# x by features from the host, latents turned off TensorE, early products with v: one kernel of a hybrid encoder trunk

## What is computed

```python
for l in range(DEPTH):                                   # DEPTH = 2
    h = rms_norm(x, norm_g[l])
    p = h @ w_in[l]                                      # 2048 x (2048 + 2112 + 2176 + 6144)
    ...                                                  # A) stick-breaking attention, 4 heads
    c_q, c_kv, k_rope, mg = split_cols(p_mla, (Q_LORA, KV_LORA, MLA_ROPE, MLA_WIDTH))
    q = (rms_norm(c_q, mla_q_norm_g[l]) @ mla_w_uq[l])   # B) latent attention: latents 512 wide
    kv = (rms_norm(c_kv, mla_kv_norm_g[l]) @ mla_w_ukv[l])
    ...
    prev = jnp.pad(rw_main, ((0, 0), (1, 0), (0, 0)))[:, :-1]
    rw_main = rw_main + rw_mu[l] * (prev - rw_main)      # C) RWKV-7: mixes each token with the one before
    rr, rk, rv, wd, ad = split_cols(rw_main, (RW_WIDTH,) * 3 + (DECAY_LORA, ICL_LORA))
    ...                                                  # per head: state <- state*w + sa*b + v*k; out = state.r
    merged = (g_sb * (y_sb @ w_br_sb[l]) + g_mla * (y_mla @ w_br_mla[l]) + g_rw * (y_rw @ w_br_rw[l]))
    x = x + merged @ w_out[l]
```

## Time and profile before

| | us |
|---|---|
| median of 3 runs | 1691.61 |
| lowest, highest | 1690.33, 1692.4 |
| the profiled execution, its own time | 1692.25 |
| its span, first to last instruction | 1690.5 |
| TensorE busy | 1677.6 |
| VectorE, ScalarE, GpSimd busy | 1134.9, 836.6, 487.8 |

### The profile page before, as it was taken

The page is one execution under the profiler, slowest core; times in us unless marked ns, Lnnn a source line. Parts: engine busy times, 40 slices in busy tenths (PEclk is TensorE's granted clock), DMA queues, the critical chain, the costliest instruction groups (busy, mean ns, idle before and its releaser), DMA issues.

```text
span 1690.5 us, 22088 instructions
## 1 busy us (share of the span) xinstructions
PE 1677.6 (99%) x8394; PEld 1399.2 (83%) x8394; DVE 1134.9 (67%) x1579; ACT 836.6 (49%) x1181; POOL 487.8 (29%) x722
## 2 busy tenths in 40 slices
PE   8999999999999999999999999999999999999999
PEld 7878888888888888888888788888888888888887
DVE  5668575766976566886656775756669666578853
ACT  6454453435544455554454454434445554555532
POOL 1011212410343426362410112233203534244500
PEclk9999999999999999999999999999999999999999
DMA  8865655655666557785687555556556565668754
GB/s 277 243 193 182 175 177 170 184 165 173 178 184 176 173 164 234 236 302 188 205 269 226 176 186 172 187 152 188 174 167 178 167 178 177 192 212 279 267 193 157
DMA packets 176913, 332.82 MB, mean 197 GB/s; under 512 B 19516, under 2 KB 32746, under 8 KB 176808
## 3 DMA queue, kind: packets, MB, share of 16 engines
q1 hardware_dynamic: 167048, 297.86, 57.7%
q0 software_dynamic: 9584, 33.48, 5.7%
q10 hardware_dynamic: 176, 0.07, 0.0%
HBM read 311.20 MB, written 16.78 MB: 194 GB/s over the span
## 4 chain that ended last, share of the span: by engine, by line
PE 92%; DVE 3%; ACT 2%; DMA 2%; issue 1%; SPq 1%; ACTq 0%; DVEq 0%
PE D L707 83%; PE B L707 8%; DMA ring<-in_w_in 2%; DVE w_lo L1398 1%; ACT w_hi L1026 1%; DVE xy L1398 0%; ACT arena L1026 0%; ACT gev L1026 0%; PE B L898 0%; DVE arena L1398 0%; DVE gev L1444 0%; PE B L877 0%; SPq L435 0%; ACT L1026 0%; DVE arena L1428 0%
## 5 line engine op out<-in xcount | busy, mean ns | idle before, releaser
L1398 DVE TENSOR_TENSOR w_lo<-ring,w_hi 128x1024 fp32r<-128x1024 f32 (+3 forms) x560 | 675.7, 1219 | 342.1 <-ACT w_hi L1026 334.0
L1026 ACT ACTIVATE w_hi<-ring 128x1024 fp32r<-128x1024 f32 (+3 forms) x560 | 575.0, 1038 | 463.9 <-PE D L707 361.5
L707 PE MATMUL D<-w_hi,ht_hi 128*128 128x512 f32 (+2 forms) x1728 | 681.3, 394 | 3.0 <-DVE w_lo L1398 2.8
L707 PE MATMUL D<-w_hi,ht_lo 128*128 128x512 f32 (+2 forms) x1728 | 666.0, 385 | 0.0
L707 PE MATMUL D<-w_lo,ht_hi 128*128 128x512 f32 (+2 forms) x1728 | 665.1, 385 | 0.0
L707 PEld LDWEIGHTS D<-w_hi,ht_hi 128*128 128x128 f32 x1728 | 325.1, 188 | 71.4 <-issue 7.8
L707 PEld LDWEIGHTS D<-w_hi,ht_lo 128*128 128x128 f32 x1728 | 324.5, 188 | 65.3
L707 PEld LDWEIGHTS D<-w_lo,ht_hi 128*128 128x128 f32 x1728 | 325.2, 188 | 59.0 <-issue 0.5
L609 POOL COPY arena<-arena 32x256 f32<-32x256 f32 x240 | 163.1, 680 | 144.7 <-DVE arena L1428 109.3
L707 PEld LDWEIGHTS B<-arena 128*66 128x66 f32 (+3 forms) x1312 | 134.2, 165 | 24.3 <-issue 8.2
L707 PE MATMUL B<-arena 128*66 128x64 f32 (+7 forms) x1312 | 144.7, 263 | 0.6 <-ACT arena L1026 0.6
(11 more groups left out here) (160 smaller groups left out, 1376.9 us busy)
## 6 DMA issues: line engine op xcount, KB each, us to landing
ring<-in_w_in SPq DMA_DIRECT2D x368, 512.0 KB, 4.5
ring<-in_w_out SPq DMA_DIRECT2D x64, 512.0 KB, 5.2
ring<-in_w_br_mla SPq DMA_DIRECT2D x32, 512.0 KB, 5.2
gate_spill<-gev POOLq DMA_DIRECT2D x24, 512.0 KB, 4.7
arena<-gate_spill POOLq DMA_DIRECT2D x24, 512.0 KB, 5.2
ring<-in_mla_w_ukv SPq DMA_DIRECT2D x16, 512.0 KB, 4.0
ring<-in_w_br_rw SPq DMA_DIRECT2D x16, 512.0 KB, 5.2
ring<-in_w_br_sb SPq DMA_DIRECT2D x16, 512.0 KB, 5.2
```

Source lines behind the costliest of these rows:

```text
L707: return nc.tensor.matmul(o, a, b, start=start, stop=stop, skip_group_check=True)
L1026: return nc.scalar.activation(o, i, fn, **kw)
L1398: return v.tensor_tensor(o, a, b, op)
```

## The change

Four things, in one kernel.

1. **x by features.** The host passes x transposed as well (`xt`) and the gains as columns (`gain_cols`). SyncE loads the four blocks of `xt` at the place of x; ScalarE and VectorE make ht_hi and ht_lo straight from them. TensorE's 32 transposes and its product with the gains go. x by rows, needed for the squares and the residual, is loaded ahead of chunks 9 to 12, and the squares stand behind the splits of chunks 12 to 15. `AT_LORA` is 17 instead of 16.
2. **Latents turned by VectorE and GpSimd.** Behind the normalising, VectorE transposes c_q and c_kv within blocks of 32 x 32 (two instructions), GpSimd moves the blocks to their places with 32 copies in groups of four (`move_latents`), during pairs 1 and 2, and ScalarE and VectorE split them ahead of pair 3 (`latents_hi`, `latents_lo`). TensorE's 16 transposes a layer go, with its wait before pair 1.
3. **Early products with v.** They are issued in the second visit of the last level, into B[0] and a part of B[3]; ScalarE copies the first half's there. A pair has 20 visits instead of 21, and the steps are spread anew.
4. **Transfers.** The rows of gains and the low-rank matrices are loaded ahead of chunk 20 instead of 12 (both layers), the constants by GpSimd after the shift of rk instead of after that of wk.

```diff
 AT_MIX = [END[n] + 3 for n in ("rr", "rk", "rv")]
-AT_LORA = END["wk"] + 8
+AT_LORA = END["wk"] + 9
...
-RW_STEPS = [1, 1.2, 1, 1.5, 1.8] + [0.88, 0.98] * LEVELS + [0.85] * 6
-LATENT_STEPS = [2, 2.5]
+RW_STEPS = [1, 1.2, 1, 1.5, 1.8] + [0.9, 1] * LEVELS + [0.98] * 5
+LATENT_STEPS = [1.2, 1.1, 1.3, 1.2]
...
-STEPS = RW_STEPS + LATENT_STEPS + 3 * RW_STEPS + GN_STEPS + ML_STEPS + SBH // 2 * SB_STEPS
+STEPS = RW_STEPS + LATENT_STEPS[:2] + 2 * RW_STEPS + LATENT_STEPS[2:] + RW_STEPS + GN_STEPS + ML_STEPS + SBH // 2 * SB_STEPS
...
         at_mkv = used[0]
+        XT = [arena[:, j * 1024:(j + 1) * 1024] for j in range(3)] + [arena[:, at_mkv:at_mkv + 1024]]
+        XT = [t.rearrange("p (k t) -> p k t", k=4) for t in XT]
         CQ, CKV = again(at_mkv, lambda: halved(1024), lambda: halved(1024))
+        LAT_TURNED = [S1, PV[:, :, 512:1024]]
+        LAT_MOVED = [t.rearrange("p h c -> p (h c)").rearrange("p (k t) -> p k t", k=4) for t in (CQ, CKV)]
...
             for j in range(4):
-                first_x(j)
+                sp.dma_start(XT[j], xt[j].rearrange("p (k t) -> p k t", k=4)).then_inc(xt_in[j], 16)
...
+                    if l == 0 and 2 * RING < n <= 3 * RING:
+                        first_x(n - 2 * RING - 1)
...
                         row(MU[:, 0:1536], rw_mu[l, 0:1536], mu_in[1][l])
-                    if n == 3 * RING:
+                    if n == 5 * RING:
...
                 shift(PW, WK[:, :, 64:192], wk_shift[l])
-                if l == 0:
-                    pool.wait_ge(split_lo, END["wk"] + 2)
-                    pool.dma_start(con[:, P:K_END], consts[:, P:K_END]).then_inc(con_in, 16)
                     shift(PV[:, :, i * 512:(i + 1) * 512], R[:, :, i * 512:(i + 1) * 512], r_shift[i][l])
+                    if l == 0 and i == 1:
+                        pool.dma_start(con[:, P:K_END], consts[:, P:K_END]).then_inc(con_in, 16)
...
+                def move_latents(i, d):
+                    turned = LAT_TURNED[i].rearrange("p h (k j t) -> p h k j t", k=4, j=4)
+                    moved = LAT_MOVED[i].rearrange("p k (h i t) -> p h k i t", h=2, i=4)
+                    if d == 0:
+                        pool.wait_ge(lat_turned, 2 * l + i + 1)
+                    for i0 in range(4):
+                        j = (i0 + d) % 4
+                        nc.gpsimd.tensor_copy(moved[32 * j:32 * j + 32, :, :, i0, :],
+                                              turned[32 * i0:32 * i0 + 32, :, :, j, :]).then_inc(lat_quarters, 1)
+                    pool.wait_ge(lat_quarters, 16 * (2 * l + i) + 4 * d + 4)
+                    if d == 3:
+                        pool.sem_inc(lat_moved, 1)
                 for p in range(4):
-                    if p == 1:
-                        beat(len(LATENT_STEPS))
+                    if p in (1, 3):
+                        beat(2)
...
                     pool.wait_ge(rw_pool, 4 * RW_POOL * l + RW_POOL * p + 7)
+                    if p in (1, 2):
+                        move_latents(p - 1, 0)
                         beat(2)
+                        if p in (1, 2):
+                            pool.wait_ge(rw_pool, 4 * RW_POOL * l + RW_POOL * p + 7 + n)
+                            move_latents(p - 1, n)
+                    if p in (1, 2):
+                        move_latents(p - 1, 3)
...
                     beat(6)
-                    beat(6)
+                    beat(5)
...
                     pe.wait_ge(rw_dve, 4 * RW_DVE * l + d0)
-                if p == 1:
-                    pe.wait_ge(lat_out[l], 16)
...
                     pe.wait_ge(rw_act, 4 * RW_ACT * l + a0 + 1 + n)
+                    if n == LEVELS:
+                        for h in range(HALVES):
+                            v = R[:, h, 1024 + p * P:1024 + (p + 1) * P]
+                            for a in range(2):
+                                mm((B[0], B[3])[h][:, h * P + 64 * a:h * P + 64 * a + 64], AM[:, 2 * a + h, 256:384],
+                                   v[:, 64 * a:64 * a + 64], a == 0, True)
...
                     if h:
-                        mm(B[0][:, 0:P], TT[:, 1, 0:P], ST, True, False)
-                    for a in range(2):
-                        last = mm(B[0][:, own[a]], AM[:, 2 * a + h, 256:384], v[:, own[a]], h + a == 0, True)
-                    last.then_inc(rw_pe, 1)
-                    beat()
+                        mm(B[3][:, P:2 * P], TT[:, 1, 0:P], ST, False, True).then_inc(rw_pe, 1)
+                        beat()
...
-            def latents():
-                beat()
-                pe.wait_ge(rw_dve, 4 * RW_DVE * l + RW_DVE)
-                pe.wait_ge(lat_dve[l], 1)
-                for i, s in enumerate((CQ, CKV)):
-                    for k in range(4):
-                        for h in range(HALVES):
-                            o = B[2 * i + k // 2][:, k % 2 * 256 + h * P:k % 2 * 256 + (h + 1) * P]
-                            last = nc.tensor.transpose(o, s[:, h, k * P:(k + 1) * P], ident)
-                    last.then_inc(lat_pe[l], 1)
-                beat()
...
-            pe.wait_ge(id_in, 16)
                 if l == 0:
-                    pe.wait_ge(gain_rows, 16)
-                    mm(D[3][:, 0:KD], NG16, ident[0:KD, 0:KD], True, True).then_inc(gain_columns, 1)
-                    for j in range(4):
-                        pe.wait_ge(x_moved[j], 16)
-                        if j >= 2:
-                            pe.wait_ge(first_xl, 2 * j - 2)
-                        transposes((2 * j, 2 * j + 1), j * 512, first_pe)
-                        if j:
-                            dense_to(2 * j)
+                    dense_to(END["wk"])
+                    pe.wait_ge(id_in, 16)
...
                     beat()
+                    if n == LEVELS:
+                        act.wait_ge(rw_pe, 4 * RW_PE * l + e + 2 * LEVELS + 2)
+                        f(YU[:, 0:P], B[0][:, 0:P]).then_inc(rw_act, 1)
                 for h in range(HALVES):
-                    for k in range(2):
-                        act.wait_ge(rw_pe, 4 * RW_PE * l + e + 2 * LEVELS + 3 + 3 * h + k)
-                        f(YU[:, k * P:(k + 1) * P], B[k][:, 0:P]).then_inc(rw_act, 1)
+                    for k in range(1 - h, 2):
+                        act.wait_ge(rw_pe, 4 * RW_PE * l + e + 2 * LEVELS + 2 + 3 * h + k)
+                        f(YU[:, k * P:(k + 1) * P], B[1][:, 0:P] if k else B[3][:, P:2 * P]).then_inc(rw_act, 1)
...
                 f(css, css, ACT.Exp, scale=-0.5).then_inc(lat_act[l], 1)
-                beat()
+                beat(2)
+            def latents_hi():
+                act.wait_ge(small_in[l], gains(l))
                 for i, (t, g) in enumerate(((cqh, cqg), (ckh, ckg))):
-                    act.wait_ge(lat_pe[l], i + 1)
-                    act.wait_ge(small_in[l], gains(l))
+                    act.wait_ge(lat_moved, 2 * l + i + 1)
                     for k in range(4):
-                        f(t[:, k, :], B[2 * i + k // 2][:, k % 2 * 256:(k % 2 + 1) * 256], scale=g[:, k:k + 1]
-                          ).then_inc(lat_hi[l], 1)
-                beat()
+                        f(t[:, k, :], LAT_MOVED[i][:, k, :], scale=g[:, k:k + 1]).then_inc(lat_hi[l], 1)
+                    beat()
...
                 if l == 0:
-                    first_split(0)
-                    columns_hi(0, first_pe, first_xh)
-                    first_split(1)
-                    columns_hi(1, first_pe, first_xh)
-                    first_split(2)
-                    first_squares(0)
-                    dense_to(1)
-                    first_squares(1)
-                    columns_hi(2, first_pe, first_xh)
-                    dense_to(3)
-                    first_squares(2)
-                    columns_hi(3, first_pe, first_xh)
-                    dense_to(5)
-                    first_squares(3, 4)
-                    dense_to(6)
-                    first_squares(5, 6)
-                    dense_to(7)
-                    first_squares(7)
-                    at[0] = END["wk"]
-                    split(END["wk"] + LEAD - 1)
+                    for c in range(KD // KC):
+                        first_columns_hi(c)
+                        if c < LEAD:
+                            first_split(c)
+                        else:
+                            dense_to(c + 1 - LEAD)
+                    dense_to(END["wk"] - 1)
+                    while at[0] < END["wk"] + 5:
+                        at[0] += 1
+                        split(at[0] + LEAD - 1)
+                        if at[0] > END["wk"] + 1:
+                            first_squares(2 * (at[0] - END["wk"]) - 4, 2 * (at[0] - END["wk"]) - 3)
...
                         latents()
+                    if p == 3:
+                        latents_hi()
...
                         last = v.tensor_scalar(t[:, h, :], t[:, h, :], css[:, 2 * i + h:2 * i + h + 1], None, ALU.mult)
-                last.then_inc(lat_dve[l], 1)
-                beat()
+                link(last)
```

(26 more changed lines are left out.)

79 lines of the change are left out of this document (39 added, 40 removed).

## The result

The changed kernel takes 1696.72 us (median of 7 runs, 1696.26 to 1699.2), the kernel before 1691.93 us in the same comparison. The ratio is 1.0034, with a 95% interval of 1.0023 to 1.0045: it is slower by 0.34% (the two medians alone give 0.28%). The profiled execution has a span of 1695.6 us, 5.1 us more than before.

The account below looks back on a forecast made before the run. TensorE bounds the kernel, so only its work or waits in the first 37 us count: -3.6 - 0.3 - 0.6 + 6.4 = +1.9 us, giving a median of 1693.5 us; range 1687.5 to 1697.0, the forecast's own 1690.3 to 1695.0.

Parts of the forecast that it names:

- The chain of the start: Layer 0's start: late squares delay GpSimd's shift, VectorE's mixing and TensorE's transposes, so chunk 17 begins at 57.0 us.
- GpSimd and VectorE in the pairs: Latent copies on GpSimd and normalising, turning and splitting on VectorE during the pairs: masks not late, price 0.
- L: Time at which chunk 12 of the weights has landed: 35.0 us, between 33 and 37.7; 34.1 before.
- So the start costs 6.4 us: Layer 0's start: chunk 17 begins at 57.0 instead of 50.6 us, and nothing later gives the 6.4 us back.
- The rule for a quick shift: Rival at the latents' shift: last transfer lands in 2 us, start costs 2.9 us, total 1690.0 us; chance 0.05.
- the 2.6 us for the rows: Queue ahead of chunk 12: no longer carrying the rows and low-rank matrices was taken to save 2.6 us.
- the queue is behind: Rival at the start: x loads delay chunk 12 to 37.7 us, start costs 9.1 us, total 1696.2 us; chance 0.21.
- the fast rival: Start: shift holds TensorE up only a little, 1688.1 us, or 1687.1 with no wait left there; chance 0.20.
- The transposes of the latents: Pairs: taking the 16 transposes off TensorE saves 1.8 us a group, 3.6 us over two layers.
- the early products: Pairs: products with v issued in the last level's visit save one visit per pair, 0.3 us in all.
- The late masks as a rival: Pairs: GpSimd's copies make level masks late by 1 us at 8 places, total 1701 us; chance 0.04.
- prelude: Early layer 1: moving the rows and low-rank matrices removes TensorE's waits at chunks 11 and 12, saving 0.6 us.

Follow-up runs that it names:

- e1: The changed kernel with 15 unused 512-column products on TensorE between chunk 16 and layer 0's latent transposes; 1696.24 us, ratio 1.0027.
- e11: The changed kernel with the start of before, GpSimd's copies later, one step number changed, rows and matrices ahead of chunk 24; 1686.94 us, ratio 0.9972.
- e10: e6 with the rows of gains and low-rank matrices loaded ahead of chunk 24, not 20; 1685.64 us, ratio 0.9965.
- e7: The changed kernel with the rows of gains and low-rank matrices loaded ahead of chunk 12 again, both layers; 1700.29 us, ratio 1.0051.
- e4: The changed kernel with GpSimd's groups of latent copies one place later, the first behind the first level mask; 1696.77 us, ratio 1.0031.
- e8: The changed kernel without the early products: products with v again in visits of their own, same sum of steps; 1698.03 us, ratio 1.0038.
- e2: The changed kernel with the squares behind the splits of chunks 9 to 12, their sum, root and wk copy earlier; 1692.04 us, ratio 1.0000.
- e5: The changed kernel with x by rows, latents' mixing and transposes two chunks later, squares behind splits of chunks 11 to 14; 1691.9 us, ratio 1.0000.
- e6: e5 plus the edit of e4 and one group-norm step number changed so the sum is 174.5 again; 1687.81 us, ratio 0.9977.
- e3: The changed kernel with the latents' mixing and their four transposes two chunks later; 1692.51 us, ratio 1.0006.

## Why the prediction was wrong

The forecast was no change that can be told, 1693.5 us, and the kernel is measurably slower, at 1696.72 us. The chain of the start was right, and the sum was 3.2 us short. Two steps failed: the cost of the standstill at the start, 1.2 us short, and the price of 0 for GpSimd and VectorE in the pairs, which was 1.2 us. What stands behind the pairs was not in the sum and cost 0.6 us.

**The start: the cost of a standstill was taken as its length.** L = 35.4 us (forecast 35.0), squares done 9.7 us behind it (9.8), first issue at L + 13.0 (13.3), landing at L + 19.3 (20.2), chunk 17 at 56.56 us (57.0). All these steps held within 1 us. The failed one is "So the start costs 6.4 us, and as TensorE is full from there on, nothing later gives them back": it counts the products behind the wait at the speed of those before it. They ran at 1.2 GHz for a while, which cost 1.7 us more, as e1 shows. 5.9 us to the begin of chunk 17 (before: 50.7 us) and 1.7 behind it are the 7.57. The Trainium skill, "TensorE: Matmul & The Clock Gate", section "What's actually happening", has the array's clock at 1.2 GHz when idle and 2.4 GHz when busy. The trace agrees, with steps of 0.43 and 0.23 us. That rule spoke against this change, and the prediction did not weigh it.

**The rule for a quick shift** did not hold for the transfer in question: the last one of the latents' shift, 0.5 KB, took 4.9 us in the changed kernel and 3.7 (e11) to 5.5 us in the others; the last one of rr's shift, 2 KB, took 10.4 us in e10. The Trainium skill ("DMA: Bandwidth & Descriptors", "Anatomy of one DMA — SWDGE (gpsimd) path") gives 2.0 us for such a size. The nearest here are other pieces of that shift, 112 KB in 2.5 us and 15 KB in 2.6 us, both in e7.

**The queue.** Chunk 8 landed at 21.15 us and not at 20.3, and the 2.6 us for the rows were 3.6 us (e7). From chunk 8 to chunk 12 lie 14.2 us; of these 12.2 - 3.6 = 8.6 are left of before, so x by rows took 5.6 us (forecast 5.4). The two errors, 0.9 us late and 1.0 us of gain too few, cancel, so that L came out right is in part luck. The rival "the queue is behind" did not occur as it was told, since it needed L at 36.5 us or more. It named the time nearly to the microsecond (1696.2) for another reason, which is luck. The two times of the fast rival don't go by the same terms: 1687.1 us leaves out the 2.0 us that 1688.1 counts.

**The transposes of the latents.** Of their 1.8 us a layer 1.7 are there: e4 has the pairs at 1.87 us less than before, with 0.2 of it for the early products (e8; forecast 0.15). The step that failed is "GpSimd and VectorE in the pairs ... Their price is 0". I had looked at the mask on GpSimd, which is not late. (Of the two waits in the earlier trace rows only the 6.8 us is ahead of a mask; the 5.2 us is ahead of an issue that waits for ScalarE.) The price came from VectorE's own chain, slowed by the copies beside it: 0.6 us a layer. The late masks as a rival had the place and not the mechanism.

**Behind the pairs.** Nothing was forecast; the half chunk by which one visit moved costs 0.57 us a layer, and smaller waits that went, at 385 and 460 us of before and at their like in layer 1, gave about 0.6 us back in all. Of the early part of layer 1 0.53 of 0.6 us came: the waits at chunks 11 and 12 went, and one of 0.15 us stands at 871.57 us, chunk 9.

**The sum again**, in microseconds: start +7.57, pairs -3.74 and +1.23 for the copies, prelude -0.53, masks behind the pairs +1.15, smaller waits -0.6: +5.1.

**x by features** itself was given 0. The times of e10 and e11 do not contradict it, and do not show it either.

## To carry to other kernels

A wait of TensorE of some microseconds can be paid twice, once as idle time and once in the slow products behind it: both belong in the sum. A step that is moved off the engine that bounds the kernel must be laid where the engines that receive it do not run a serial chain that the bound engine waits for; the check is on each neighbour's chain, not on its own queue alone. And where positions come from a running sum that is cut to a grid, list all positions before and after: 0.3 more in a sum of 174.5 steps moved a visit by half a chunk, hundreds of microseconds further on.

## What the runs showed of the hardware

TensorE's clock behind a wait is not a function of the wait's length alone: behind 2.07 us at chunk 11 it fell in e2, and behind 2.33 us at the same place it stayed in the changed kernel. Behind 1.77 us near 66 us it fell in e5, and behind 1.76 us near 65 us it stayed in e6. It fell behind those of 3.62, 3.78, 2.88 and 2.79 us at the transposes (the changed kernel, e4, e8, e7) and of 3.07 us at chunk 11 in e7. Where it fell, TensorE had in most cases already worked again at 2.4 GHz for about 1 to 1.5 us (the changed kernel, e1, e2, e3, e5). So one execution's start says only within 1 to 2 us what the next one's is.

Operations of VectorE on SBUF became longer beside copies by GpSimd, and those longer too: 0.69 to 0.88 us for a 128x512 product, 2.76 (e4, where they stand apart) to 4.05 us for four copies. The Trainium skill ("SBUF — State Buffer", section "Who interferes with whom") has an instruction of VectorE with two inputs in SBUF contend with one of GpSimd that reads SBUF, and calls the port pair that they share an exclusive lock. The direction agrees. Here a copy takes about 0.7 us alone, and a VectorE operation of the chain grew by 0.1 to 0.2 us, so the rows show less than a wait for a whole copy.

The time to land of a small transfer that GpSimd issues here goes little by its size. The last one of the latents' shift, 0.5 KB, took 3.7 to 5.5 us and the last one of rr's shift, 2 KB, 5.5 to 10.4 us, while the 448 KB that lead rr's shift took 4.7 to 9.0 us beside them.
